# Two decoder blocks on one core: VectorE makes the low parts of a weight chunk in one operation of 2,048 columns

## What is computed

```python
def first_block(...):                       # stick-breaking attention, then the MLP
    a = rms_norm(h, norm_mix[i])
    h = h + stick_breaking_mixer(a, sb_w_qkv[j], sb_w_o[j])
    h = h + sq_relu_mlp(rms_norm(h, norm_mlp[i]), mlp_w1[i], mlp_w2[i])
    return rms_norm(h, final_norm)

def second_block(...):                      # 16 meta tokens are put in front of the 256
    proj = rms_norm_2(h, norm_mix_g) @ w_in
    ...                                     # pooling and convolution branches, gates, w_o
    gate, up = jnp.split(rms_norm_2(h, norm_ffn_g) @ w_gate_up, 2, axis=-1)
    h = h + (jax.nn.silu(gate) * up) @ w_down
    return rms_norm_2(h, norm_final_g)[:, N_META:]
```

## Time and profile before

| | before |
|---|---|
| median of three runs | 2454.61 us |
| the profiled execution: its own time | 2454.94 us |
| its span, first to last instruction | 2453.2 us |
| busy share of the span: TensorE, VectorE, ScalarE, GpSimd | 100%, 67%, 49%, 6% |
| mean granted TensorE clock | 1.000 |

### The profile page before, as it was taken

The page is one execution under the profiler, slowest core; times in us unless marked ns, Lnnn a source line. Parts: engine busy times, 40 slices in busy tenths (PEclk is TensorE's granted clock), DMA queues, the critical chain, the costliest instruction groups (busy, mean ns, idle before and its releaser), DMA issues.

```text
span 2453.2 us, 39643 instructions
## 1 busy us (share of the span) xinstructions
PE 2448.2 (100%) x15839; PEld 2273.1 (93%) x15839; DVE 1652.5 (67%) x1415; ACT 1206.5 (49%) x1185; POOL 142.7 (6%) x87
## 2 busy tenths in 40 slices
PE   9999999999999999999999999999999999999999
PEld 9999999999999999999999999999999889988998
DVE  7677777656656666787765886666766556665665
ACT  5456555444444444544543344544554544444444
POOL 0001100000000000000200630000000000000001
DMA  8655556666666666565656566666666565666664
GB/s 267 200 174 170 172 189 202 196 203 205 196 199 205 199 198 203 190 204 190 205 191 203 191 201 196 203 206 200 195 205 201 192 200 196 204 204 200 197 221 138
DMA packets 243960, 485.34 MB, mean 198 GB/s; under 512 B 7728, under 2 KB 8944, under 8 KB 243696
## 3 DMA queue, kind: packets, MB, share of 16 engines
q1 hardware_dynamic: 243520, 483.12, 59.9%
q10 hardware_dynamic: 320, 0.53, 0.1%
HBM read 481.53 MB, written 2.10 MB: 197 GB/s over the span
## 4 chain that ended last, share of the span: by engine, by line
PE 99%; DMA 0%; issue 0%; DVE 0%; SPq 0%; ACT 0%
PE ps L1365 44%; PE ps L1372 23%; PE ps L1420 12%; PE ps L1399 8%; PE ps L1428 6%; PE ps L1405 4%; PE ps L1476 0%; PE ps L1442 0%; PE ps L1530 0%; DMA raw<-in_sb_w_qkv_dram 0%; PE ps L1464 0%; PE ps L1605 0%; PE ps L1513 0%; PE ps L1535 0%; PE ps L1467 0%
## 5 line engine op out<-in xcount | busy, mean ns | idle before, releaser
L810 DVE TENSOR_TENSOR wlo<-raw,whi 128x1024 fp32r<-128x1024 f32 x900 | 1144.8, 1284 | 750.7 <-ACT whi L602 749.3
L602 ACT ACTIVATE whi<-raw 128x1024 fp32r<-128x1024 f32 x900 | 947.8, 1056 | 1154.1 <-PE ps L1372 815.7
L1365 PE MATMUL ps<-b_buf,whi 128*128 128x512 f32 x2816 | 666.3, 379 | 0.0
L1365 PEld LDWEIGHTS ps<-b_buf,whi 128*128 128x128 f32 x2816 | 506.3, 190 | 56.6
L1372 PEld LDWEIGHTS ps<-b_buf,wlo 128*128 128x128 f32 x2816 | 369.0, 191 | 18.9
L1372 PE MATMUL ps<-b_buf,wlo 128*128 128x256 f32 x2816 | 371.1, 275 | 0.0
L1365 PE MATMUL ps<-c_buf,whi 128*128 128x512 f32 x1280 | 303.0, 380 | 0.0
L1420 PE MATMUL ps<-a_buf,whi 128*128 128x258 f32 (+4 forms) x2304 | 282.2, 276 | 1.1 <-issue 1.1
L1420 PEld LDWEIGHTS ps<-a_buf,whi 128*128 128x128 f32 x2304 | 269.6, 191 | 1.6 <-issue 1.3
L1365 PEld LDWEIGHTS ps<-c_buf,whi 128*128 128x128 f32 x1280 | 230.1, 190 | 25.7
L1365 PE MATMUL ps<-a_buf,whi 128*128 128x512 f32 x896 | 211.9, 379 | 0.0
(11 more groups left out here) (204 smaller groups left out, 1374.6 us busy)
## 6 DMA issues: line engine op xcount, KB each, us to landing
raw<-in_mlp_w_dram SPq DMA_DIRECT2D x128, 1024.0 KB, 5.2
raw<-in_w_in_dram SPq DMA_DIRECT2D x96, 1024.0 KB, 5.1
raw<-in_w_gate_up_dram SPq DMA_DIRECT2D x88, 1024.0 KB, 5.0
raw<-in_sb_w_qkv_dram SPq DMA_DIRECT2D x44, 1024.0 KB, 5.1
raw<-in_w_down_dram SPq DMA_DIRECT2D x44, 1024.0 KB, 5.1
raw<-in_sb_w_o_dram SPq DMA_DIRECT2D x16, 1024.0 KB, 5.2
raw<-in_conv_out_w_dram SPq DMA_DIRECT2D x16, 1024.0 KB, 5.1
raw<-in_w_o_dram SPq DMA_DIRECT2D x16, 1024.0 KB, 5.1
```

Source lines behind the costliest of these rows:

```text
L602: act.activation(whi[:, unit_of(n, u)], raw[:, n % RAW, u * UK:(u + 1) * UK, :], ACT.Copy).then_inc(w_hi, 1)
L810: dve.tensor_tensor(wlo[:, s], raw[:, n % RAW, u * UK:(u + 1) * UK, :], cast(whi[:, s]), ALU.subtract).then_inc(w_lo, 1)
L1365: pe.matmul(ps[:, 4 * half + j, :].rearrange("p (c n a) -> p c n a", c=2, a=2), whi[:, unit_of(n, u), kt, j * P:(j + 1) * P], parts_by_tur ...
```

## The change

`split_lo` on VectorE issues one operation for a chunk instead of two for its units. It waits for both high parts (`w_hi` at the chunk's second unit), subtracts over 2,048 columns at once and counts `w_lo` up by two. `chunk_of` gives the chunk's two units in the ring as one run of columns. ScalarE's `split_hi` stays as it is, unit by unit; so do the first panel's `split_unit` on both engines, all of TensorE's waits, and the evacuations. The 42 matmuls at TensorE's end go.

```diff
+        def chunk_of(part, n):
+
+            s = unit_of(n, 0)
+            return part[:, s:s + UNITS].rearrange("p s t n -> p (s t n)")
...
                 dve.wait_ge(raw_landed[n % RAW], landed_count(cnt, ahead))
-                for u in range(UNITS):
-                    dve.wait_ge(w_hi, cnt.at("chunk", ahead) * UNITS + (u + 1))
-                    s = unit_of(n, u)
-                    dve.tensor_tensor(wlo[:, s], raw[:, n % RAW, u * UK:(u + 1) * UK, :], cast(whi[:, s]),
-                                      ALU.subtract).then_inc(w_lo, 1)
+                dve.wait_ge(w_hi, cnt.at("chunk", ahead) * UNITS + UNITS)
+                dve.tensor_tensor(chunk_of(wlo, n), raw[:, n % RAW].rearrange("p t n -> p (t n)"),
+                                  cast(chunk_of(whi, n)), ALU.subtract).then_inc(w_lo, UNITS)
...
             run(pe, cnt, body)
 
-            row = d_hi.rearrange("p t n -> p (t n)")
-
-            def spare(i, stationary, moving, n):
-
-                pe.matmul(ps[:, 2 + i % 2, 0:n], stationary, moving, start=True, stop=True, skip_group_check=True)
...
-            for i in range(6):
-                spare(i, block(0), by_turns(d_hi[:, i, :]), T)
...
```

More of the change, by code:

```diff
@@ L1599, in _ @@
             run(pe, cnt, body)
-            row = d_hi.rearrange("p t n -> p (t n)")
-            def spare(i, stationary, moving, n):
-                pe.matmul(ps[:, 2 + i % 2, 0:n], stationary, moving, start=True, stop=True, skip_group_check=True)
-            def block(i):
-                return whi[:, i // 8, i // 4 % 2, i % 4 * P:(i % 4 + 1) * P]
-            for i in range(6):
-                spare(i, block(0), by_turns(d_hi[:, i, :]), T)
[L1613 to L1624, removed]
 _INS = ["x", "meta_tokens_2", "norm_mix", "norm_mlp", "final_norm", "sb_w_qkv", "sb_w_o", "mlp_w1", "mlp_w2",
```

## The result

The changed kernel takes 2463.88 us (median of six runs, 2463.50 to 2464.20), the kernel before in the same runs 2454.73 us: 9.15 us more, a ratio of 1.0037 with a 95% interval of 1.0026 to 1.0048. It is slower, by 0.37%; forecast were 2462.9 us and a range of 2457 to 2467.5.

What follows compares the result with a forecast made beforehand. The prediction took TensorE, busy 2448.2 of 2453.2 us, to bound the kernel. Seven places where it would wait for late VectorE work summed to 8.29 us; 2454.61 + 8.3 gave 2462.9 us, range 2457 to 2467.5.

Steps and rivals of the forecast that it cites:

- place 2: VectorE's `weights_lo` in attention groups 0, 1 and 2: 1.06 us each on top of the existing wait, 3.18 us.
- place 3: Attention group 3: its low part comes 1.03 us late for chunk 54, costing TensorE 0.55 us.
- place 4: Chunk 56: the PSUM half it needs is freed late by VectorE's evacuation, 0.75 us.
- place 5: The norm between the blocks: it and the TensorE waiting for it come 0.86 us late.
- chunks 210 and 455: Low parts late for TensorE: 1.50 us at chunk 210, behind the evacuation with most operations; 0.39 at 455, the last chunk.
- The cover of 3.6 us: Inside panels, 3.6 us of slack remain before TensorE needs a low part, so nothing happens there.
- Group 0's suffix sums: Attention group 0: GpSimd's mask ends 1.34 us after a late pair, with no slack, costing TensorE 1.06 us.
- chunk 56: TensorE waits for a PSUM half that an evacuation frees late: 0.75 us.
- chunk 54: TensorE waits for group 3's late low part at this chunk: 0.55 us.
- Chunk 198: After the norm: no cost if the evacuation's PSUM read runs beside GpSimd's operation, otherwise 0.9 us more.
- Not slower: Rival: VectorE is mostly behind, not waiting for the second high part, so pairs save time: 2454.2 us; chance 0.19.
- Worse: Rival: suffix sums of groups 1 to 3 also late, PSUM operation at chunk 198 stands: 2467.0 us; chance 0.08.

Runs made afterwards that it cites:

- experiment 2: The changed kernel with its wait for both high parts kept, but two operations of 1,024 columns instead of one: 2463.36 us, ratio 1.0034 to the kernel before.
- experiment 3: The changed kernel, with one operation per chunk only where an evacuation or attention step stands behind, the others unit by unit: 2462.84 us, ratio 1.0033.
- experiment 4: The changed kernel, unit by unit where an evacuation or attention step stands behind, one operation per chunk everywhere else: 2456.77 us, ratio 1.0008.
- experiment 9: The changed kernel with the evacuation ahead of the pair at the close of unpaired k, v and projection panels: 2458.92 us, ratio 1.0015.
- experiment 5: The changed kernel without VectorE's wait for the weight DMA in `split_lo`: 2463.91 us, ratio 1.0036 to the kernel before.
- experiment 7: The changed kernel with an unused 1,024-column reduction on VectorE ahead of the pair where a panel's evacuation follows: 2484.43 us, ratio 1.0119.

## Why the prediction was right

**The operation.** Forecast 2.29 us, and 2.20 to the next start; measured 2.29 and 2.21. By this the Trainium skill's rule for float32 `tensor_tensor` (VectorE: DVE Perf Modes, the TRN2 errata) agrees with the trace. Its advice to make tiles large held for VectorE's busy time and failed for the kernel: the advice counts the engine's own time and no wait. VectorE's busy time fell by 93.8 us (1652.5 to 1558.7; the low parts by themselves 101.1) rather than by the 30 to 70 that I named. Of the 101, 60 are start-up: two small ones apart take 2 x 1.225 us, one pair 2.29, so that a pair whose halves didn't follow each other directly saves 0.16 us and not the 0.07 of the prediction. The other 41 come from low parts that were stretched beside GpSimd: before, 43 of them took 54.4 us more than usual, after, 18 took 13.3 more.

**The wait.** Everything that stands behind a pair comes one low part later; experiments 2 to 4 and 9 bear this out, each against its rival. The terms of places 2 to 5 were undersized by 0.03 to 0.13 us each. At chunks 210 and 455 the first load came 0.11 and 0.10 us later than forecast as well, and the next one gave that back, so these two terms hit by luck. The part shared by most is the 0.07 to 0.10 us by which the pair starts later behind the high part (experiment 5); I had taken the 0.03 of the small one.

**Inside panels** hardly anything happened: TensorE waited at three of 450 pairs (26, 210 and 455). The prediction allowed 210 and 455 only, and named a wait in the middle of a panel as a sign of being wrong. Chunk 26, the third of its panel, is such a wait, of 0.55 us; like 210 it is made behind an evacuation that came late. The cover of 3.6 us held for the other pairs, and one place where it doesn't was left out.

**Group 0's suffix sums** were oversized: 1.06 forecast, 0.70 measured. I let GpSimd's masks end 1.34 us behind the pair, as before. They ended 0.62 behind it (151.35 + 4.39 = 155.74, the pair ended 155.12), since GpSimd got in during the 0.32 us in which VectorE waited for ScalarE: the first of its four masks ended at 152.61, in that pause, where before it ended at 154.26, behind both low parts (153.99). Of the 0.70, 0.55 came at chunk 26's low part, a place that the prediction doesn't name; by its own figures (the pair ends at 155.05, the trace of before wants it at 154.91) it would have been 0.19.

**Two places were missing**, 0.24 and 0.44 us: chunk 226, where a one-chunk panel frees the half, and the last stage, whose short panels leave the last `up` tile little slack. Both are of the class that I had priced at chunk 56 and chunk 54, and the prediction looks for it in panels of four chunks only. The missing places and the undersized terms make the sum 1.2 us too small; the oversized term and the start of the kernel, 0.3 us shorter in this execution, take 0.66 us of that back. That the sum is only 0.55 us short is luck to this extent.

**Chunk 198** went as worked out, with less room. The changed kernel's VectorE and GpSimd there:

```profile
1087.14 1.23 DVE L1018 TENSOR_TENSOR U<-ps,rr 128x1032 f32<-128x1032 f32 x1
1088.40 2.16 DVE L1024 TENSOR_TENSOR S<-U 128x1028 f32<-128x1028 f32 x1
...
1091.73 2.28 DVE L813 TENSOR_TENSOR wlo<-raw,whi 128x2048 fp32r<-128x2048 f32 x1
...
1085.13 4.33 POOL L1248 TENSOR_TENSOR h<-h,rr 128x1024 f32 x1 [681.00 <-DVE rr L973]
...
1094.27 0.97 PEld L1431 LDWEIGHTS ps<-a_buf,wlo 128*128 128x128 f32 x8
```

The operation that reads PSUM (L1018) took its 1.23 us beside GpSimd's, the next, with both inputs in SBUF, 2.16 instead of 1.23. By that the rule of the Trainium skill (SBUF — State Buffer, Who interferes with whom) agrees with the trace. The pair was done at 1094.01, 0.26 us before it was wanted; the prediction had 0.41.

**The rivals.** Not slower (0.19): the case that VectorE is behind anyway is real, at the norm, but rare; most of its pairs stood waiting for ScalarE (366 of 450). Worse (0.08): the suffix sums of groups 1 to 3 kept their slack at one dose, and lost it at two (experiment 7). The removed matmuls were worth nothing.

## What to carry to other kernels

Before two operations are joined behind the later of their two inputs, look at what stands behind them in the engine's queue: it comes later by the length of the first operation, which used to lie in the wait, and the first result comes later by the distance of the two inputs. An engine's busy share says nothing about it; the price is read at the few places where the bound engine has less slack than that, and these are found by going through every kind of wait that it has, short panels and stage ends too. If the joined operation is wanted all the same, what needn't wait for its inputs goes ahead of it in the queue, and what is moved ahead must be followed to its own next consumer.

## What the runs showed of the hardware

- TensorE's clock fell behind waits of 2.69 to 2.73 us, four times in one execution (experiment 7), and cost 1.4 to 1.7 us each; behind waits of up to 1.9 us it stayed at 1.00. In the changed kernel, with 1.63 us at most, it costs nothing.
- A `tensor_tensor` of 2,048 columns behind one wait started 0.10 us behind the end of the operation that it waited for (360 of 364 cases), one of 1,024 columns 0.03 (337 of 337). Behind two waits it was 0.10 or 0.13 and 0.03 or 0.10. What makes the difference is open.
